# Token halves around the third norm of a two-layer transformer kernel, and a new order of splits, squares and half tiles around the second

## The reference, cut to what matters

```
x = rms_norm(x + gate * (merged @ w_out), final_g)      # first layer's end: blocks o0..o7
z = rms_norm_2(h, g_mix_pre) @ w_in_2                   # "second norm": blocks Ecb0, Eca0, ...
mix = concat(y_conf, y_att, y_sc, y_pool) @ w_out_2     # blocks x0..x7
h = h + rms_norm_2(mix, g_mix_post)                     # "third norm"
hn = rms_norm_2(h, g_mlp_pre)                           # its own norm of h (norm number 4)
ff = square(relu(hn @ w_up)) @ w_down                   # blocks u0_0..u7_3 and d0_0..d7_3
h = h + rms_norm_2(ff, g_mlp_post)
gate = sigmoid(rms_norm_2(h, g_ple_pre) @ w_ple_gate)   # blocks g0..g7
```

## Time and profile before

| | us |
|---|---|
| median of three runs | 2678.51 |
| the profiled execution's own time | 2678.38 |
| its span in the trace | 2676.6 |
| PE busy | 2531.2 (95%) |
| DVE busy | 954.3 (36%) |
| ACT busy | 832.2 (31%) |
| POOL busy | 856.7 (32%) |
| mean granted clock of PE | 0.971 |

### The profile page before, as it was taken

One profiled execution on the slowest core, in us unless ns is written; L12 is line 12 of the kernel. 1 busy time (PEld: TensorE's weight loads), 2 busy tenths in 40 slices (PEclk: granted clock), 3 DMA queues, 4 the chain that ended last, 5 costly groups with the idle time before them and its releaser, 6 DMA issues.

```text
span 2676.6 us, 30174 instructions
## 1 busy us (share of the span) xinstructions
PE 2531.2 (95%) x12612; PEld 1965.2 (73%) x12612; DVE 954.3 (36%) x1242; ACT 832.2 (31%) x1233; POOL 856.7 (32%) x414
## 2 busy tenths in 40 slices
PE   7999999999998989999999999989999999999896
PEld 4877778656686656788787667878888888888775
DVE  6324330455304555202278575031122222222423
ACT  4104541454423545313323433242111111112321
POOL 2212112443322112235532211453323333234632
PEclk8989999999998999999999999989999999999898
DMA  7101011000020000013121000201111111111111
GB/s 303 48 24 48 30 34 49 31 28 19 25 83 30 11 21 15 22 59 103 40 102 40 24 24 30 110 24 48 48 48 48 55 48 41 53 49 48 46 40 73
DMA packets 34582, 135.35 MB, mean 51 GB/s; under 512 B 3664, under 2 KB 4112, under 8 KB 33040
## 3 DMA queue, kind: packets, MB, share of 16 engines
q1 hardware_dynamic: 34128, 132.38, 14.2%
q10 hardware_dynamic: 320, 1.05, 0.2%
HBM read 123.97 MB, written 8.39 MB: 49 GB/s over the span
## 4 chain that ended last, share of the span: by engine, by line
PE 85%; DVE 5%; issue 4%; POOL 3%; ACT 2%; DMA 1%; SPq 0%; POOLq 0%; ACTq 0%; DVEq 0%
PE slot L770 57%; PE slot L818 13%; PE ps L1064 2%; PE ps L1040 2%; PE ps L1025 2%; PE ps L868 1%; POOL wlo L1756 1%; PE ps L1050 1%; PE ps L1129 1%; PE ps L1118 1%; PE ps L1095 1%; PE ps L1107 1%; DVE ada_sum L2379 1%; DMA ada<-wada 1%; DVE sklo L2268 1%
## 5 line engine op out<-in xcount | busy, mean ns | idle before, releaser
L770 PE MATMUL slot<-xhi,whi 128*128 128x512 f32 x2192 | 723.1, 409 | 35.7 <-DVE xlo L2543 16.9
L1756 POOL TENSOR_TENSOR wlo<-raw,whi 128x1024 fp32r<-128x1024 f32 (+1 forms) x169 | 433.0, 2562 | 836.7 <-ACT whi L1321 836.7
L770 PE MATMUL slot<-xlo,whi 128*128 128x512 f32 x2192 | 694.7, 396 | 0.0
L770 PE MATMUL slot<-xhi,wlo 128*128 128x512 f32 x2192 | 691.7, 395 | 0.0
L770 PEld LDWEIGHTS slot<-xhi,whi 128*128 128x128 f32 x2192 | 403.2, 192 | 153.3 <-issue 68.1
L770 PEld LDWEIGHTS slot<-xlo,whi 128*128 128x128 f32 x2192 | 419.7, 191 | 91.6
L770 PEld LDWEIGHTS slot<-xhi,wlo 128*128 128x128 f32 x2192 | 418.6, 191 | 91.7
L1321 ACT ACTIVATE whi<-raw 128x1024 fp32r<-128x1024 f32 (+1 forms) x169 | 186.3, 1102 | 298.4 <-PE slot L818 174.2
L1538 ACT ACTIVATE ptr<-ps 128x256 f32<-128x256 f32 (+3 forms) x176 | 79.9, 454 | 274.1 <-PE ps L1040 273.9
L818 PE MATMUL slot<-uhi,whi 128*128 128x512 f32 x512 | 158.3, 390 | 0.0
L818 PE MATMUL slot<-ulo,whi 128*128 128x512 f32 x512 | 157.8, 389 | 0.0
(11 more groups left out here) (346 smaller groups left out, 2768.2 us busy)
## 6 DMA issues: line engine op xcount, KB each, us to landing
raw<-wstream SPq DMA_DIRECT2D x129, 512.0 KB, 3.3
raw<-wstream SPq DMA_DIRECT2D x40, 640.0 KB, 3.9
ada<-wada SPq DMA_DIRECT2D x7, 1024.0 KB, 20.1
mm<-xT SPq DMA_DIRECT2D x2, 2048.0 KB, 9.9
ada<-wada SPq DMA_DIRECT2D x2, 2048.0 KB, 27.1
mm<-xT SPq DMA_DIRECT2D x8, 512.0 KB, 3.9
res_dram<-mm SPq DMA_DIRECT2D x8, 512.0 KB, 3.0
res<-res_dram SPq DMA_DIRECT2D x8, 512.0 KB, 7.3
```

The source lines that it names most:

```text
L770: o = mm_(outs[:, half * HALF:(half + 1) * HALF], w[b % 2][:, k_w, :], x[:, k_x, half * HALF:(half + 1) * HALF], start=first and j == 0, s ...
L1756: tt(flat(wlo[b % 2])[:, 0:n], (raw1 if b == 1 else raw)[:, 0:n], flat(whi[b % 2])[:, 0:n].bitcast(F32), ALU.subtract).then_inc(w_lo, 1)
```

## The change

What it does, part by part:

- Third norm by halves: x6 and x7 are computed for the first 512 tokens, then for the second; half sums, half rows, and for each half eight chunks of scaling (DVE), residual (POOL), `xhi` and square (ACT), `xlo` (DVE). On ACT and POOL the first three chunks of half one come ahead of x7's second half, then the split of u0_1's weights, then chunks 3 to 7.
- u0_0 and u0_1 by halves. PE's order: parts 0 and 1 of u0_0, the third norm's second half sums around parts 2 and 3, then u0_1's parts 0 to 3 with two sums, then both blocks' parts 4 to 7 with a half sum behind each pair, and the row of the second half behind the fifth half sum (counting from 0, number 4); then the second half in the same way. The row of the fourth norm stands before the last two half parts of u0_1.
- The squares of the fourth norm are summed by halves: sixteen half sums (`half_chunk_sum`), into `ps6`.
- The weights of o7 and x7 are split at the last part of o5 and x5, ahead of the squares of that tile on ACT and the adds on POOL (before: behind them).
- Around the second norm POOL's adds of o6's second half move behind its `xlo` of chunks 1 and 3; Ecb0's first half does four parts, not two, before the sums; the first four parts of the second halves of Ecb0 and Eca0 alternate; the split of Ecb1's weights moves to the fifth part of Eca0's second half.

The core of the diff:

```diff
-OPENERS = [("Dv0", "Dv1"), ("u0_0", "u0_1")]
+OPENERS = [("Dv0", "Dv1")]
-SECOND = {b for _, b in OPENERS} | {"g1", "Eca0"}
+SECOND = {b for _, b in OPENERS} | {"g1", "Eca0", "u0_1"}
+LAST_WHOLE = ("o5", "x5")
+def halves_around_norm3():
+    out = half_events("x6", 0) + half_events("x7", 0)
+    ev = half_events("x6", 1)
+    out += [("nsum3", 0, 0)] + ev[:4] + [("nsum3", 0, 1)] + ev[4:]
+    ev = half_events("x7", 1)
+    out += ev[:2] + [("nrow3", 0)] + ev[2:] + [("nrest3",)]
+    a, b = half_events("u0_0", 0), half_events("u0_1", 0)
+    q = [("hsum3", n) for n in range(2 * NC)]
+    out += a[:2] + [("nsum3", 1, 0)] + a[2:4] + [("nsum3", 1, 1)] + b[:2] + q[:1] + b[2:4] + q[1:2]
+    for n in range(4, 8):
+        out += [a[n], b[n], q[n - 2]] + ([("nrow3", 1)] if n == 6 else [])
+    a, b = half_events("u0_0", 1), half_events("u0_1", 1)
+    for n in range(4):
+        out += [a[n], b[n], q[n + 6]]
+    out += a[4:5] + q[10:12] + a[5:6] + q[12:13] + a[6:7] + q[13:14] + a[7:] + q[14:]
+    return out + b[4:6] + [("hrow", 4)] + b[6:]
...
-    out += ev[:2] + [("nsum2", 1, 0)] + ev[2:5] + [("nsum2", 1, 1)] + ev[5:]
+    out += ev[:4] + [("nsum2", 1, 0)] + ev[4:6] + [("nsum2", 1, 1)] + ev[6:]
...
-    return out + half_events("Ecb0", 1) + half_events("Eca0", 1)
+    first, second = half_events("Ecb0", 1), half_events("Eca0", 1)
+    return out + [ev for two in zip(first[:4], second[:4]) for ev in two] + first[4:] + second[4:]
...
+            def norm3_high(half, n):
+                c, q = slice(half * HALF, (half + 1) * HALF), half * NC + n
...
+                nc.scalar.activation(xhi[:, n, c], res[:, n, c], ACT.Copy, scale=v_("g_mlp_pre", n, 1)
+                                     ).then_inc(x_hi if half else act_half, 1)
+                if q < 3:
+                    act.wait_ge(pe_half, PE_HALF["sum3"])
+                else:
+                    act.wait_ge(pq_used, q - 2)
+                nc.scalar.activation(sring[q % 3][:, 0:HALF], res[:, n, c], ACT.Square).then_inc(pq_done, 1)
...
# ACT and POOL, each in its own walk
+                    if BLOCKS[ev[1]][1] in LAST_WHOLE and ev[2] == 7:
+                        split_weights(ev[1] + 2)
...
-                    if (name, ev[2:]) in (("o6", (0, 0)), ("Eca0", (0, 1))):
+                    if name in ("Eca0", "u0_1") and ev[2:] == (4, 1):
                         split_weights(ev[1] + 1)
-                    elif name == "o6" and ev[2:] == (7, 1):
-                        split_weights(INDEX["Ecb0"])
+                    elif name in ("o6", "x6") and ev[2:] == (7, 1):
+                        split_weights(ev[1] + 2)
...
# ACT
+                elif ev[0] == "nrow3":
+                    if ev[1]:
+                        wait_tile(act, LAST_USE[4])
+                    for n in range(8 if ev[1] else 3):
+                        norm3_high(ev[1], n)
+                    if ev[1]:
+                        std(4)
+                elif ev[0] == "nrest3":
+                    split_weights(INDEX["u0_1"])
+                    for n in range(3, NC):
+                        norm3_high(0, n)
...
# POOL
+                elif ev[0] == "nrow3":
+                    if not ev[1]:
+                        pool.wait_ge(res_in, 16 * NC)
+                    for n in range(8 if ev[1] else 3):
+                        norm3_residual(ev[1], n)
+                elif ev[0] == "nrest3":
+                    split_weights(INDEX["u0_1"])
+                    for n in range(3, NC):
+                        norm3_residual(0, n)
...
                 elif ev[0] == "nrest2":
+                    add_half_squares(1)
                     for n in (5, 7):
                         norm2_low(0, n)
                     split_weights(INDEX["Eca0"])
...
# DVE
+                elif ev[0] == "nrest3":
+                    for n in range(3, NC + 2):
+                        norm3_scaled(0, n)
+                elif ev[0] == "nrow3":
+                    dve.wait_ge(nrow, 4)
+                    for n in range(NC + 2):
+                        if n == NC:
+                            applied(3, t_ready, 8)
+                        norm3_scaled(1, n)
+                    v.tensor_copy(wide_row, rstd(4)).then_inc(napplied, 1)
+                    dve.wait_ge(napplied, 5)
```

More of the change, by code:

```diff
@@ L1712, in _ @@
                     split_weights(INDEX["Eca0"])
[L1713 to L1721, removed]
-                    for n in range(NC):
[L1723 to L1731, removed]
+                elif ev[0] == "norm4":
+                    for n in range(2):
+                        wait_evacuated(act, "d%d_%d" % (NEIGHTH - 1, NC // 2 - 1), n)
+                    std(5)
+                    wait_tile(act, LAST_USE[5])
+                    split_weights(INDEX["g1"])
+                    for n in range(NC):
+                        wait_residual(act, 1, n)
+                        nc.scalar.activation(xhi[:, n, :], res[:, n, :], ACT.Copy, scale=v_("g_ple_pre", n, 1)
+                                             ).then_inc(x_hi, 1)
+                        chunk_square(2, n, res[:, n, :])
+                    act.wait_ge(p_in, 32)
+                    for n in range(2):
+                        nc.scalar.activation(yhi[:, n, :], zs2[n][:], ACT.Copy).then_inc(y_hi, 1)
+                    std(6)
                 elif ev[0] == "norm5":
@@ L2089, in norm2_rstd, with norm3_rstd, norm3_scaled @@
                                 ).then_inc(nrstd if half else dve_half, 2 if half else 1)
+            def norm3_rstd(half):
+                c = slice(4 * half, 4 * half + 4)
+                if half:
+                    dve.wait_ge(nstd, 4)
+                else:
+                    dve.wait_ge(act_half, ACT_HALF["std3"])
+                v.reciprocal(rrms[:, 0, c], rms[:, 0, c]).then_inc(nrstd if half else dve_half, 1)
+            def norm3_scaled(half, n):
+                c = slice(half * HALF, (half + 1) * HALF)
+                if n < NC:
+                    scaled(mm[:, n, c], mm[:, n, c], v_("g_mix_post", n, 1), ps4[:, c], t_ready if half else dve_half)
+                m = n - 2
+                if m >= 0:
+                    if half:
+                        dve.wait_ge(x_hi, 32 + m + 1)
+                        done = x_lo if m % 2 else x_lo2
+                    else:
+                        dve.wait_ge(act_half, ACT_HALF["h3", m])
+                        done = dve_half
+                    v.scalar_tensor_tensor(out=xlo[:, m, c], in0=res[:, m, c], scalar=v_("g_mlp_pre", m, 1),
+                                           in1=xhi[:, m, c].bitcast(F32), op0=ALU.mult, op1=ALU.subtract
+                                           ).then_inc(done, 1)
             def norm2_scaled(half, n):
```

187 lines of the change are left out of this document (138 added, 49 removed).

## The result

| | us |
|---|---|
| before, median of four runs | 2679.75 (2675.79 to 2681.03) |
| after, median of four runs | 2703.24 (2701.30 to 2704.17) |
| ratio | 1.009, 95% interval 1.0078 to 1.0102 |
| profiled execution after: time, span, mean granted clock | 2702.57, 2700.8, 0.963 |

The change costs 0.9%, some 24 us. The forecast was 2681.5 with a range up to 2690: wrong, although it leaned to the slow side.

What follows compares the result with a forecast made beforehand. TensorE (PE), 85% of the chain, bounds the kernel, so order gains only at its idle or low clock. Third norm 8.7 us lost less second norm 5.8 gained gives +2.9 on some 2678.5: 2681.5, range 2674.5 to 2690.

Steps and rivals of the forecast that it cites:

- 5.8 forecast: Second norm, o6 to Ecb1: the change gains 5.8 us net, bounds 4 and 7.7.
- the low clock that I left in place at 1.8: Second norm, second part of Ecb0: low clock stays, as sums still stand beside four parts; 1.8 us more if it goes.
- The waits of 0.8 and 0.5: Second norm: first half sums wait 0.8 us for their sources; sums behind the moved second-half adds wait 0.5.
- 1.7, 0.8, 5.9, 1.3 and 1.7 forecast: Third norm, PE waits in us: chunk 0, chunk 1, part 3 of u0_0, second row, first chunk behind that row.
- the 5.9: Third norm, before part 3 of u0_0: PE idle 5.9 us, POOL's residual 3 standing behind u0_1's weight split.
- so 1.4 is lost: At u0_2: two half parts, not two whole, hide the fourth norm's row copy and slot reading; 1.4 us lost.
- The first group whole, 8 us, and nothing for the second.: Third norm: low clock costs 8 us from the stall to the second row, nothing in the half parts behind it.
- A: Rival, third norm: the clock comes back at once, costing 3 us; 2676.5 us in all; chance 0.27.
- C: Rival, third norm: halves hide the norm, the 5.9 wait falls to 1.5 to 2; 2672.3 us; chance 0.10.
- D: Rival, second norm: the change does not act, since the load, not the order, holds o7; chance 0.01.
- B: Rival, third norm: clock low through both groups, price 17 us; 2690, or 2686 with part of the second; chance 0.20.
- 8.7 lost: Third norm net: waits 13.5 plus clock 8 minus the 12.8 us lost before gives 8.7 us lost.

Runs made afterwards that it cites:

- norm2_alone: The kernel before with only the change's part around the second norm; 2675.16 us against 2677.84 before, ratio 0.9985.
- The early split alone: The kernel before with only o7's weights split ahead of o5's squares; 2674.44 us against 2680.03 before, ratio 0.9978.
- the rest alone: The kernel before with the second norm's later adds and sums and alternating second halves, o7's split unmoved; 2676.72 us, ratio 0.9982.
- res3_ahead: The changed kernel with residual 3 on POOL and `xhi` 3 on ACT ahead of the split of u0_1's weights; 2695.81 us, ratio 1.0063.
- split_ahead: The changed kernel with u0_2's weights split ahead of the emptying and narrowing of u0_0 on ACT and POOL; 2691.60 us, ratio 1.0042.
- both_tail: both_orders, with the second half's sums keeping the order part, part, sum up to part 5; 2681.91 us, ratio 1.0014.
- both_row: both_orders, with the second half row one group sooner, its square root and reciprocal also moved ahead; 2678.83 us, ratio 1.0001.
- both_orders: The changed kernel with the moves of split_ahead and res3_ahead together; 2686.90 us, ratio 1.0037.
- both_row_tail: both_orders with the further moves of both_row and both_tail together; 2679.24 us, ratio 0.9998.

## Why the prediction was wrong

**Second norm: the waits right, the size right in this trace and too high as a rule.** 5.8 forecast, 6.2 measured from o6 to Ecb1 (64.8 against 58.6). But seven of nine traces with the same program give 3.1 to 3.6, and the time of norm2_alone 2.7. The term that was mis-sized is the low clock that I left in place at 1.8: it was about that in the two good traces and about 5 in the seven. That the trace of the changed kernel was one of the two is luck. The waits of 0.8 and 0.5 were 0.7 and 0.3. The early split alone measured 5.1 (forecast 4.8); the rest alone 2.7 (forecast 1.1, too low by the clock that I left in place). About 2 us of it were given back ahead of x5 in the changed kernel; I had counted the whole as kept. In the profiled trace 1.5 of that is the step between the marks at 1435 and 1453, in the forgetting attention. The granted clock from 1445 to 1450 was 0.66 there and 1.00 before; nothing was tried against it.

**Third norm, the waits up to the second half: right.** 1.7, 0.8, 5.9, 1.3 and 1.7 forecast; 1.67, 0.67, 5.50, 1.08 and 1.81 measured, with the causes that were named. res3_ahead shows that the 5.9 hung on the split of u0_1 ahead of residual 3 and `xhi` 3.

**The failed step: "so 1.4 is lost" at u0_2.** It was 9.35. I asked what of the row was still hidden by PE's work, and took u0_2's weights as ready since they had been in the earlier trace rows. They were ready there because their split stood ahead of u0_0's emptying. The change moves the split, and I costed the move on PE's order, not on ACT's and POOL's own programs, where it passes `uhi` and `ulo`. With the low clock behind it this is 9.7 to 11.6 us, by split_ahead.

**The clock: the size was low and the place wrong.** "The first group whole, 8 us, and nothing for the second." The first group cost about 5, because the clock came back at 1783, sooner than the row. The second cost about 10, most of it in its tail, where the new order thins the parts between the sums; both_tail takes 5 of that back with the same instructions, 4.6 by the traces. I treated the two groups as alike (six matmuls to a sum) and did not look at the tail, whose order is written out in the diff. All six traces with that tail have a low stretch of 13 us or more there; the three with the steady order have one of 3 to 7.

**The rivals.** A (the clock back at once) and C (halves that hide) are refuted by the windows and by the 5.5. D was refuted by o7's start. B is the nearest: its price of 17 for the clock was close to the 15 measured, and with it alone the forecast would have been 2690; together with the missed 8 of the wait and the 3 of clock at u0_2 that gives 2701. That the 17 and the 15 agree is in part luck. But its mechanism holds only in part. The second row's wait and that behind it did bring the clock down again (window 1795 to 1800), and both_row took 8 us by removing them. The rule that I cited for it, from the Trainium skill ("TensorE: Matmul & The Clock Gate", "A second HAM failure mode: psum-queue depth-cycling"), is that short idles between groups cost throughput by repeated changes of the clock. The trace agrees as to the stretch behind the row (waits of 1.08 and 1.81, then 0.66 from 1795 to 1800). It does not cover the tail, where PE had no idle that the profile shows and the clock was 0.50 for 16 us.

**The sum.** Against the forecast for the third norm, 8.7 lost, stand 26.4: 8 more by the wait at u0_2, 3 by the clock behind it, 7 by the clock inside (15 and not 8). At x5 3.6 of the second norm's 5.8 were left.

The chances leaned to slower, 0.38, but the range ended at 2690: it took in the bounds of the costs that I had listed and nothing for a dependency that I had not.

## What to carry to other kernels

When a change moves a step, write out the program of every engine that issues it, and read what now stands ahead of it there: a split needs nothing but its weights, and yet it waits for all that stands ahead of it, the adds of o5 in the kernel before (4.1 us) and `ulo` in the changed one (9.35). An order that keeps sums and parts in a steady mix to the end took 3 to 5 us off the traces here, as much as a removed wait. Where the gain sought is a few us of short waits, judge it over many executions: here the clock gave or took more than that under the same instructions.

## What the runs showed of the hardware that was not expected

- The granted clock was 0.50 for some 16 us without any wait of PE that the profile shows, while single-column sums stood among few matmuls of 512 columns (changed kernel, 1810 to 1826). In the steady mix of six such matmuls to a half sum it was 0.99 and 1.00 (1800 to 1810).
- The same program with the same waits had the clock at 1.00 in one execution and at 0.50 for some 13 us in another (res3_ahead and both_orders, 1763 to 1777), 4.2 us apart at the end of the group. The same holds for work outside the change: 0.50 and 1.00 from 1645 to 1650 in both_row_tail and both_row, and 3 or 10 us of low clock behind the second norm's sums in nine traces of one program. Times of one kernel spread by as much: both_tail from 2673.5 to 2686.7. How much of that spread is the clock's isn't shown.
- POOL's `ulo`, as large as a split, took 3.44 us while DVE worked on `tbuf`; the next one, with DVE idle, took 2.38, as long as a split (2.35).
